# A hybrid decoder layer on eight cores: the first weight block through the sync queue, and a new order of the start

## The reference

```python
hn = rms_norm(h, norm_w)
proj = hn @ w_in
u, gp, q, k, v, gr = jnp.split(proj, [o1, o2, o3, o4, o5], axis=-1)
q = rotary(split_heads(q).astype(jnp.float32), pos)
k = rotary(split_heads(k).astype(jnp.float32), pos) * (HEAD_DIM ** -0.5)
```

## Time and profile before

| | us |
|---|---|
| median of 6 runs (556.08 to 560.52) | 556.54 |
| the profiled execution | 555.85 |
| its span, on its slowest core (core 6) | 554.3 |
| spans of the 8 cores | 549.7 to 554.3 |
| PE busy | 529.6 |
| DVE, ACT, POOL busy | 352.7, 184.7, 249.5 |
| HBM read and written, MB | 68.75, 30.21 |

### The profile page before, as it was taken

The page is one execution under the profiler, slowest core; times in us unless marked ns, Lnnn a source line. Parts: engine busy times, 40 slices in busy tenths (PEclk is TensorE's granted clock), DMA queues, the critical chain, the costliest instruction groups (busy, mean ns, idle before and its releaser), DMA issues.

```text
span 554.3 us, 12909 instructions; the slowest of 8 cores (549.7 to 554.3 us)
## 1 busy us (share of the span) xinstructions
PE 529.6 (96%) x4902; PEld 328.6 (59%) x4902; DVE 352.7 (64%) x577; ACT 184.7 (33%) x481; POOL 249.5 (45%) x296
## 2 busy tenths in 40 slices
PE   4799999989999999999999999999999999999994
PEld 1345456969864465665647465656647475664763
DVE  2578677615665376558647666568667567666763
ACT  1312214543762132140523333322415233222432
POOL 4214026269745026455461916364462818236130
PEclk8899999999999999999999999999999999999999
DMA  8999998678874939655986959675867958355231
GB/s 185 212 180 173 171 169 135 100 162 261 264 222 123 255 129 187 146 146 151 199 230 176 235 124 190 167 195 148 203 185 183 239 138 246 105 146 144 89 98 76
DMA packets 75880, 95.49 MB, mean 172 GB/s; under 512 B 50718, under 2 KB 53486, under 8 KB 74524
## 3 DMA queue, kind: packets, MB, share of 16 engines
q1 hardware_dynamic: 71308, 77.04, 52.6%
q0 software_dynamic: 4368, 17.37, 18.3%
q10 hardware_dynamic: 144, 0.26, 0.1%
HBM read 68.75 MB, written 30.21 MB: 179 GB/s over the span
## 4 chain that ended last, share of the span: by engine, by line
PE 79%; DMA 11%; DVE 3%; issue 2%; ACT 2%; POOL 1%; SPq 0%; POOLq 0%; DVEq 0%; ACTq 0%
PE pp L784 26%; PE pp L1041 20%; PE pp L800 14%; PE pp L853 10%; DMA b<-x 4%; DMA normw_b<-x 3%; DMA b<-w_out 2%; PE pp L638 1%; DMA Ss<-b 1%; PE pp L1111 1%; DMA b<-S_in 1%; PE pp L1127 1%; PE pp L1129 1%; PE pp L978 1%; ACT b L663 1%
## 5 line engine op out<-in xcount | busy, mean ns | idle before, releaser
L784 PE MATMUL pp<-w_in_bf,b 128*128 128x512 bf16 x768 | 173.7, 379 | 1.2 <-ACT bh L905 1.0
L679 POOL TENSOR_TENSOR small<-small,nh 128x1 f32<-128x1 f32 (+3 forms) x52 | 48.0, 927 | 190.2 <-DVE small L674 114.2
L800 PE MATMUL pp<-b,w_in_bf 128*128 128x128 bf16 x2048 | 120.4, 219 | 2.3 <-issue 1.3
L784 PEld LDWEIGHTS pp<-w_in_bf,b 128*128 128x128 bf16 x768 | 72.5, 98 | 84.3 <-issue 4.5
L800 PEld LDWEIGHTS pp<-b,w_in_bf 128*128 128x128 bf16 x2048 | 116.2, 98 | 7.3 <-issue 3.7
L1041 PE MATMUL pp<-b 128*128 128x512 bf16 (+1 forms) x528 | 114.6, 372 | 0.4 <-DVE b L1282 0.4
L1041 PEld LDWEIGHTS pp<-b 128*128 128x128 bf16 x528 | 50.3, 98 | 54.6 <-issue 0.5
L938 POOL TENSOR_TENSOR bh<-bh 128x284 f32<-128x284 bf16 (+3 forms) x85 | 77.1, 922 | 4.2 <-DVE b L942 4.1
L853 PE MATMUL pp<-w_in_bf,b 128*128 128x512 bf16 x256 | 60.4, 385 | 4.6 <-ACT w_in_bf L603 2.3
L1004 ACT ACTIVATE b<-pp 128x128 bf16<-128x128 f32 x128 | 33.2, 290 | 86.4 <-PE pp L1129 86.4
L1013 DVE SCALAR_TENSOR_TENSOR b<-pp,small,b 128x128 bf16<-128x128 f32 x128 | 34.5, 343 | 17.5 <-POOL small L679 17.5
(11 more groups left out here) (148 smaller groups left out, 585.8 us busy)
## 6 DMA issues: line engine op xcount, KB each, us to landing
b<-x SPq DMA_DIRECT2D x29, 512.0 KB, 4.9
scr<-b SPq DMA_DIRECT2D x45, 256.0 KB, 3.1
w_in_bf<-w_in POOLq DMA_DIRECT2D x8, 1024.0 KB, 22.5
b<-w_out SPq DMA_DIRECT2D x16, 512.0 KB, 5.9
b<-S_in SPq DMA_DIRECT2D x16, 512.0 KB, 5.2
Ss<-b SPq DMA_DIRECT2D x16, 512.0 KB, 3.1
y<-b SPq DMA_DIRECT2D x15, 512.0 KB, 3.1
w_in_bf<-w_ut POOLq DMA_DIRECT2D x2, 1024.0 KB, 31.8
```

Of the source, the lines that this page charges most:

```text
L679: pool(lambda e: e.tensor_tensor(out=rp.ap[:T, 0:n], in0=rs.ap[:T, 0:n], in1=nh.ap[:T, 0:n], op=ALU.pow), [rs, nh], [rp], 0.57 if n == 1 e ...
L784: r = e.matmul(pt.ap[:, nt * 512:(nt + 1) * 512], lhsT=hnT.ap[:, kc * 128:(kc + 1) * 128], rhs=win.ap[:, blk + nt, kc, :], start=(kc == 0) ...
L800: r = e.matmul(pt.ap[:, (4 * nt + fc) * T:(4 * nt + fc + 1) * T], lhsT=win.ap[:, blk + nt, kc, fc * 128:(fc + 1) * 128], rhs=hnT.ap[:, kc ...
```

## The change: what it does

- Block 6 goes over SP's queue whole, in two transfers of 1 MB (each partition 8 KB in one row) in place of two of 512 KB (4 KB). They land as f32 in the room of blocks 2 and 3 (STAGE), and four casts of 1024 columns take them into block 6. The slots wq0 and wq1 are gone.
- The two parts of block 6 leave POOL's queue. It begins with the rotary tables, x2, x4, block 11, x3, block 10; the rest is in another order too. The entries "w 3", "wu" and "w 2" stand further ahead, but are still sent in their later groups.
- The loops over HWQ and in `send` create their operations in sorted order; the priorities still come from the place in HWQ and QUEUE.
- The planner's figures: SW_FIRST 4.1 for 4.0, SP's start 1.5 for 1.0, true sizes for x1 and the weights on SP's queue, four times the bytes for the later rotary tables ("cs").
- OFFSET is another table.

```diff
-SW_RATE, HW_RATE, HW_SLOW, HW_HALF, SW_FIRST = 0.322e6, 0.26e6, 0.063e6, 0.16e6, 4.0
-START = {"pe": 1.0, "act": 1.0, "dve": 1.0, "pool": 1.5, "sp": 1.0}
+SW_RATE, HW_RATE, HW_SLOW, HW_HALF, SW_FIRST = 0.322e6, 0.26e6, 0.063e6, 0.16e6, 4.1
+START = {"pe": 1.0, "act": 1.0, "dve": 1.0, "pool": 1.5, "sp": 1.5}
 
 OFFSET = {
-    "L-1 pe:w_in_bf>fold": -170, "L-8 dve:x>hn": -136, "L-8 pool:stat>stat": -185, "L0 pe:hnT>smu": 139,
...
+    "L-8 dve:x>hn": -90, "L0 act:smu>uf": -289, "L0 dve:wost>wo": 222, "L0 pe:hnT>pjg": -600, "L0 pe:hnT>pjp": 146,
...
-    for n, (kind, k) in enumerate(HWQ):
+    for n, (kind, k) in sorted(enumerate(HWQ), key=lambda item: item[1]):
         prio = n - 980
         if kind == "x":
-            dma("hw", lambda k=k: xt[k].ap, lambda k=k: x[(k - 1) * 128:k * 128, :], [], [xt[k]], 420000, prio,
+            dma("hw", lambda k=k: xt[k].ap, lambda k=k: x[(k - 1) * 128:k * 128, :], [], [xt[k]], 1 << 19, prio,
                 "uniq" if k in XHOME else None)
         elif kind == "w":
-            wq = P.tile("b4", "wq%d" % k)
-            dma("hw", lambda wq=wq: wq.ap, lambda k=k: w_in[ORDER[0]][:, k * 1024:(k + 1) * 1024], [], [wq], 420000, prio)
-            dst = lambda k=k: win.ap[:, ORDER[0], 2 * k:2 * k + 2].rearrange("p k n -> p (k n)")
-            P.op([("act", lambda e, d=dst, wq=wq: e.activation(out=d(), in_=wq.ap, func=AF.Copy), 1.06),
-                  ("dve", lambda e, d=dst, wq=wq: e.tensor_copy(out=d(), in_=wq.ap), 0.63),
-                  ("pool", lambda e, d=dst, wq=wq: e.tensor_copy(out=d(), in_=wq.ap), 1.05)],
-                 [wq], [(win, (ORDER[0], k))], -850 + k, port=True)
+            half = lambda k=k: win.ap[:, STAGE[k]].rearrange("p k n -> p (k n)").bitcast(F32)
+            dma("hw", half, lambda k=k: w_in[ORDER[0]][:, k * 2048:(k + 1) * 2048], [], [(win, (STAGE[k], 0))], 1 << 20, prio, "uniq")
+            for j in range(2):
+                h = 2 * k + j
+                dst = lambda h=h: win.ap[:, ORDER[0], 2 * h:2 * h + 2].rearrange("p k n -> p (k n)")
+                src = lambda half=half, j=j: half()[:, j * 1024:(j + 1) * 1024]
+                P.op([("act", lambda e, d=dst, s=src: e.activation(out=d(), in_=s(), func=AF.Copy), 1.06),
+                      ("dve", lambda e, d=dst, s=src: e.tensor_copy(out=d(), in_=s()), 0.63),
+                      ("pool", lambda e, d=dst, s=src: e.tensor_copy(out=d(), in_=s()), 1.05)],
+                     [(win, (STAGE[k], 0))], [(win, (ORDER[0], h))], -850 + h, port=True)
...
     def send(*nums):
-        for n in nums:
+        for n in sorted(nums, key=lambda n: repr(QUEUE[n])):
...
-            dma("hw", lambda: cst.ap, lambda: c_cs[idx], [], [cst], 1 << 16, prio + 0.1, after=after)
+            dma("hw", lambda: cst.ap, lambda: c_cs[idx], [], [cst], 1 << 18, prio + 0.1, after=after)
...
-QUEUE = (("w", 6, 2), ("w", 6, 3), ("x", 2), ("x", 4), ("cs",), ("x", 3), ("w", 7), ("w", 10, 0), ("w", 10, 1),
-         ("w", 4), ("x0",), ("w", 11), ("w", 5), ("wp", 1), ("w", 9), ("w", 8), ("ut", 1), ("sp", 0), ("ut", 0),
-         ("wp", 0), ("wu", 7), ("wu", 3), ("wu", 4), ("wu", 5), ("wu", 1), ("sp", 1), ("wu", 2), ("wu", 0),
-         ("wu", 6), ("w", 2), ("w", 3), ("cb",))
+QUEUE = (("cs",), ("x", 2), ("x", 4), ("w", 3), ("w", 11), ("x", 3), ("w", 10, 0), ("w", 10, 1), ("w", 4), ("w", 7),
+         ("x0",), ("w", 5), ("wu", 1), ("w", 8), ("w", 9), ("wp", 0), ("wp", 1), ("ut", 1), ("ut", 0), ("wu", 3),
+         ("wu", 4), ("wu", 5), ("wu", 2), ("sp", 1), ("sp", 0), ("w", 2), ("wu", 7), ("wu", 0), ("cb",), ("wu", 6))
```

More of the change, by code:

```diff
@@ L24 @@
 SEM_LAT = 0.12
-SW_RATE, HW_RATE, HW_SLOW, HW_HALF, SW_FIRST = 0.322e6, 0.26e6, 0.063e6, 0.16e6, 4.0
-START = {"pe": 1.0, "act": 1.0, "dve": 1.0, "pool": 1.5, "sp": 1.0}
+SW_RATE, HW_RATE, HW_SLOW, HW_HALF, SW_FIRST = 0.322e6, 0.26e6, 0.063e6, 0.16e6, 4.1
+START = {"pe": 1.0, "act": 1.0, "dve": 1.0, "pool": 1.5, "sp": 1.5}
 OFFSET = {
[7 rows of a table removed]
[L36 to L43, removed]
[10 rows of a table added]
+    "act:pjg>G": 177, "act:u>uw": -9, "act:x>stat": -99, "dve:pjq>q": 70, "dve:stat>stat": -587,
+    "last pe:W>ret": -107, "last pe:hnT>pjq": -496, "last pe:hnT>pju": -107, "last pe:kT>sc": -97,
+    "last pe:q>tr": -7, "last pe:yr>out": -199, "pe:KQ>dSs": -600, "pe:Sb>retS": -35, "pe:aux>ssY": 250,
+    "pe:hnT>pjg": 60, "pe:hnT>pjq": 11, "pe:hnT>pju": 56, "pe:hnT>pjv": 73, "pe:k>dS": -600, "pe:kT>sc": -382,
+    "pool:V>Rh": 469, "pool:stat>stat": -76, "pool:winA>winB": 64, "pool:winB>pooled": 467, "pool:winB>winA": 600,
+    "sp:q>scr": -330, "sp:scr>qT": -122, "sp:w_in_bf>Sin": -256,
 }
```

## The result

The changed kernel takes **560.29 us** (median of 10 runs, 557.64 to 650.4); the kernel before, run beside it, 556.80 (20 runs). The ratio is **1.0059, 95% interval 1.0035 to 1.0082**: slower by 0.6%. It stands over runs in which no die ran at a lower clock than the other. I had forecast 554.2, faster. The profiled execution took 558.78 us, with spans of 550.2 to 557.2 us on the eight cores. Lines 853, 800, 784, 743 and 1041 of before are 857, 804, 788, 747 and 1045 now.

The account below looks back on a forecast made before the run. The prediction took TensorE (PE), busy 96% of the span, as the bound: 555.85 us profiled, less 1.5 at the start and 0.8 from the new order, is 553.55; with the median 0.69 higher, 554.2 us, range 550 to 560.

Parts of the forecast that it names:

- The sorts: Loops over HWQ and in send: only ties shift, since priorities keep their old place; 0 us.
- the casts: Four casts of block 6 instead of two, on DVE or ACT: up to 1.4 us if DVE took both, taken as 0.
- the bounds: Whole kernel: PE is busy 96% of the span; the end is its work, its late start and the tail.
- Block 6 over SP: Start, SP's queue: 8 KB rows cost near twice 4 KB ones; con about 13.7 us, block 6 cast at 21.2.
- POOL's queue: Start: without block 6, x2 lands about 16 us, x4 about 20.7, block 11 near 28, x3 near 29.5.
- PE with these: PE's start: no gap from x4's first matmul at 26.4 us; 21.1 us lost against 22.65, so 1.5 us won.
- does the gain last to 49 us?: PE after the start: later blocks land as before; a gain up to 4 us meets no starved PE.
- The new offsets and estimates: PE's order from 28.3 to 546.7 us: at most 4.6 us to win, as much to lose; 0.8 won taken.
- the new order waits elsewhere: Rival, PE's order: a table made for a start the chip doesn't give costs 3 to 4 us, 559.5; chance 0.08.
- The half block: Rival, start: block 6's second half lands too late and holds PE's queue; about 4 us slower, 560.5; chance 0.12.
- nothing comes of it: Rival, start: x4 gains what con and block 6's second half lose; 555.5 to 556.5 us; chance 0.15.
- The sum: Whole kernel: 555.85 - 1.5 - 0.8 = 553.55, the median 0.69 above the profiled run, so 554.2 us.

Follow-up runs that it names:

- e6_rows4k: The changed kernel with each 1 MB half of block 6 read as two transfers with rows of 4 KB on the same queue; 562.37 us, 1.0104.
- e14_order_alone: e3_shift with five moves in the written order of POOL and TensorE and two on VectorE, casting reads as in the changed kernel; 554.83 us, 0.9958.
- e3_shift: The changed kernel with 64 more small matmuls (half a page of code) in TensorE's idle time at the start; 556.03 us, 0.9989.
- e12_before_shift: The kernel before with 36 small matmuls (72 instructions) at the start; 558.52 us, 1.0027.
- e5_shift256: The changed kernel with 128 more small matmuls (256 instructions, a whole page of code) in the idle time of the start; 559.93 us, 1.0048.

## Why the prediction was wrong

*The sorts, the casts, the bounds.* Nothing contradicts them: PE bound the kernel, and the end was its work, its start and its waits.

*Block 6 over SP.* Con was forecast near 13.7 and came at 13.35; the whole block at 21.2 and came at 20.2, when ACT's last cast ended. A packet of 8 KB took SP 0.40 to 0.44 us at 12 to 17 us, one of 4 KB 0.20 to 0.25 in e6_rows4k, near twice as I had taken; e6_rows4k shows that the width carries the gain. The rule of the Trainium skill that I weighed there ("Issuing engines are not separate DMA queues"), by which this would be 0, said nothing of the width of rows, which decided here, by e6_rows4k.

*POOL's queue.* The order of arrivals was as forecast, the times too late. ACT's squares of x2, x4 and x3 in the changed kernel, core 5, and all its DMA of 8 to 17 us:

```profile
13.48 1.06 ACT L714 ACTIVATE b<-S_f 128x1024 bf16<-128x1024 f32 x1 [0.68 <-DMA S_f<-x]
18.13 1.06 ACT L714 ACTIVATE b<-finw_b 128x1024 bf16<-128x1024 f32 x1 [3.50 <-DMA finw_b<-x]
26.39 1.06 ACT L714 ACTIVATE b<-normw_b 128x1024 bf16<-128x1024 f32 x1 [6.16 <-DMA normw_b<-x]
...
DMA packets 656, 2.63 MB, mean 292 GB/s; under 512 B 78, under 2 KB 206, under 8 KB 497
```

x2, x4 and x3 came 2.5 to 3.1 us before my 16, 20.7 and 29.5. The mis-sized number is the rate: I used 255 KB/us, and it was 292. From 8 us to x4's 20.7 that makes 12.7 x (1 - 255 / 292) = 1.6 us, an estimate, of x4's 2.6; the rest I can't say.

*PE with these; does the gain last to 49 us?* The dense run began at 24.9 (26.4), 2.6 us were won (1.5), and no block starved PE from then up to 98 us. Right in kind, too small; but the path was another. I had the dense run wait for x4's norm; x4's first projections began at 21.65, and the run at 24.93 waited 1.37 us for the DMA of a weight block.

*The new offsets and estimates.* **This step failed.** I took 0.8 us won and wrote that as much as 4.6 could be lost again; 5.6 were, give or take some 1.5 (changed kernel against e14_order_alone). Two things were in it, parted by the ratios of e3_shift and e14_order_alone. Some 1.7 us are waits of the new order, the rival "the new order waits elsewhere", which I had priced at 3 to 4 us and given 0.08. The other 3.9 us, the stop for the code page and the half clock behind it, are no wait of an order at all, and no rival of mine had them. The new order put 256 short instructions right behind the end of the folding, where the casting reads are released, and the page border happened to fall there. My sentence that what was lost at 100 to 130 lay in x5's 17.4 us was wrong in part: some of that stretch is pages already in the kernel before, where three cores stop for 1.3 to 1.8 us at 1979 (core 6, the slowest, for 1.3).

*The other rivals.* The half block was not late here; with rows of 4 KB in e6_rows4k it was. And nothing near "nothing comes of it": 2.6 us did come, and went.

*The sum.* 2.6 us won and 5.6 lost is 3.0 lost; measured 3.5 by the medians, 3.3 by the ratio. With pages and waits mostly out of the way, e14_order_alone stands at 554.8, where 557.3 less the start's 2.6 is 554.7. The two agree better than their intervals (0.8 us either way for e14_order_alone) let one claim, and in part by luck: its profiled start is some 0.8 us later than the changed kernel's, and page stops are in both it and the kernel before.

*What stays open.* I can't say why a page asked for at the same time comes at 93.6 on one core and at 100.2 on another: on core 5 the DMA engines were busy for only 0.29 of the time from 94 to 95 us, with the border crossed at 91.9, and the page still had not started. In e3_shift four cores got a page 7.3 to 8.0 us after the border at about 85 us, at 91.8 to 93.7, when block 3's first rows (from 93.3) had hardly begun. POOL's queue carried other reads then (on core 0 it had 0.92 of the engines from 86 to 92 us), so block 3's rows are not all that can delay a page. Why the hold of 1.4 us did harm is open too.

## What to carry to other kernels

A re-plan that changes nothing but order can move a code page's border to where bulk reads begin: when a stop has no semaphore behind it, count the engine's instructions and look at the queue that carries code. Half a page of small instructions at the start is a cheap probe, if it stands where the engine is idle anyway; in e12_before_shift it stood between work, and the start came later. Take written-order waits away one after the other before judging them, since the first one hides the next.

## What the runs showed of the hardware

- Stops named "issue" stand at the same counts of TensorE's instructions in all kernels here: 699, 1467, 1723, 1979, 2235, multiples of 256 apart, with weight loads, matmuls and waits for semaphores counted (some ten less on cores where records are missing). The Trainium skill says so ("Runtime: NRT & Kernel Launch", section "Instruction fetch mechanics"): code comes in blocks of 16 KiB, 256 instructions, by a DMA queue of the engine's own. Its sentence that the cost of a border is "mostly hidden" does not hold here: up to 4.1 us, and the clock's 2.6 behind them.
- A page waits behind rows of a casting read: with those of block 3 in front it took 8.3 us from border to packet (91.9 to 100.2), with rows a quarter as long 2.4 to 5.2 us on six cores, with the read held for 5 us 2.3 to 5.1.
- Behind 4.1 us without a matmul the granted clock was 0.50 for at least 3.4 us. Not every stop does that: behind 2.0 us on core 4 of the changed kernel, and behind 3.2 us on core 2 of e5_shift256, it stayed 1.00.
- Rows of 8 KB on SP's queue beside POOL's reads: 292 GB/s at 8 to 17 us, where with rows of 4 KB 704 packets moved 2.38 MB in the same 9 us, 264 GB/s. In both the queues moved about equal numbers of packets (335 and 321; 356 and 348), so the wider rows got more of the bytes.
